# State copies of a decoder step in 56 pieces, released by the latent decode and by the last MLP

## What is computed

```python
def reference(x_prompt, x_sample, state_conv, state_swa0, state_swa1, state_swa2, state_pool, cache_mla, page_table, ...):
    for i in range(DEPTH):
        ...
        xp = xp + g1p * yp
        xs = xs + g1s * ys
        xp = xp + g2p * sq_relu_mlp(modulate(xp, norm2_g[i], sh2p, sc2p), mlp_w1[i], mlp_w2[i])
        xs = xs + g2s * sq_relu_mlp(modulate(xs, norm2_g[i], sh2s, sc2s), mlp_w1[i], mlp_w2[i])

def swa_decode(h, bufs, w_qkv, qn_g, kn_g, w_o):
    ...
        kf = jnp.concatenate([buf[:, :, 0].astype(k.dtype), k[:, :, g]], axis=1)
        vf = jnp.concatenate([buf[:, :, 1].astype(v.dtype), v[:, :, g]], axis=1)
        ...
        keep = min(w, lb + s)
        states.append(jnp.stack([kf[:, lb + s - keep:], vf[:, lb + s - keep:]], axis=2))
```

## Time and profile before

| what | value |
|---|---|
| median of 3 runs | 2119.54 us |
| lowest and highest run | 2116.04 and 2130.07 us |
| the profiled execution, its own time | 2127.36 us |
| its span, first to last instruction | 2125.8 us |
| TensorE (PE) busy | 1928.3 us, 91% |
| VectorE (DVE), ScalarE (ACT), GpSimd (POOL) busy | 1122.3, 779.5, 23.8 us |
| mean granted clock of TensorE | 0.94 of full speed |
| moved by DMA | 408.74 MB, of which 60.28 by GpSimd's queue |

### The profile page before, as it was taken

How to read it: one execution, slowest core, us unless ns; L and a number is a source line. 1 busy time by engine, 2 the same in 40 slices (tenths; PEclk the granted TensorE clock), 3 DMA queues, 4 the chain that set the end, 5 groups by cost and what they waited for, 6 DMA issues and landing times.

```text
span 2125.8 us, 32739 instructions
## 1 busy us (share of the span) xinstructions
PE 1928.3 (91%) x12829; PEld 1663.7 (78%) x12829; DVE 1122.3 (53%) x1869; ACT 779.5 (37%) x1515; POOL 23.8 (1%) x44
## 2 busy tenths in 40 slices
PE   5999999999997789999869999896899797789997
PEld 2876999989985559999749999743599696579997
DVE  4365554459744456543475544487556363365542
ACT  2312543244423234432224433343246363145432
POOL 0000000000000000000000000000000000000000
PEclk7999999999988999999989999996799898799999
DMA  9666666643441995656636656431058787434442
GB/s 358 238 238 219 220 216 218 218 158 120 165 182 50 405 335 187 230 205 218 209 116 235 212 211 209 169 103 52 1 176 291 240 268 231 149 117 144 154 149 74
DMA packets 227862, 408.74 MB, mean 192 GB/s; under 512 B 9944, under 2 KB 208639, under 8 KB 210689
## 3 DMA queue, kind: packets, MB, share of 16 engines
q1 hardware_dynamic: 223888, 341.08, 46.6%
q0 software_dynamic: 2384, 60.28, 8.3%
q10 hardware_dynamic: 1449, 5.39, 0.7%
HBM read 400.67 MB, written 60.28 MB: 217 GB/s over the span
## 4 chain that ended last, share of the span: by engine, by line
PE 72%; DVE 10%; SPq 6%; DMA 6%; issue 3%; ACT 3%; POOL 0%; ACTq 0%; DVEq 0%; POOLq 0%
PE bank L1163 40%; PE bank L1069 12%; PE bank L1138 3%; PE bank L1082 3%; DMA work<-in_pages_rope 3%; SPq L574 3%; DMA work<-in_keys_turned 2%; PE bank L1277 2%; DVE rstd L1818 2%; PE bank L1549 2%; SPq L577 2%; SPq L567 1%; DMA work<-in_ada_w 1%; PE bank L1034 1%; PE bank L1326 1%
## 5 line engine op out<-in xcount | busy, mean ns | idle before, releaser
L1673 DVE TENSOR_TENSOR ring_lo<-ring,ring_hi 128x1024 fp32r<-128x1024 f32 (+1 forms) x324 | 380.1, 1214 | 338.3 <-ACT ring_hi L715 338.3
L715 ACT ACTIVATE ring_hi<-ring 128x1024 fp32r<-128x1024 f32 (+1 forms) x324 | 323.2, 1046 | 300.9 <-PE bank L1163 283.2
L1163 PE MATMUL bank<-hidden_hi,ring_hi 128*128 128x320 f32 x1024 | 319.2, 312 | 0.0
L1163 PE MATMUL bank<-hidden_hi,ring_lo 128*128 128x320 f32 x1024 | 316.4, 309 | 0.0
L1163 PE MATMUL bank<-hidden_lo,ring_hi 128*128 128x320 f32 x1024 | 316.3, 309 | 0.0
L1163 PE MATMUL bank<-h_hi,ring_hi 128*128 128x320 f32 x896 | 279.9, 312 | 0.1
L1163 PE MATMUL bank<-h_lo,ring_hi 128*128 128x320 f32 x896 | 276.3, 308 | 0.0
L1163 PE MATMUL bank<-h_hi,ring_lo 128*128 128x320 f32 x896 | 275.9, 308 | 0.0
L1163 PEld LDWEIGHTS bank<-hidden_hi,ring_hi 128*128 128x128 f32 x1024 | 192.2, 188 | 22.6 <-issue 22.6
L1163 PEld LDWEIGHTS bank<-hidden_lo,ring_hi 128*128 128x128 f32 x1024 | 192.3, 188 | 0.0
L1163 PEld LDWEIGHTS bank<-hidden_hi,ring_lo 128*128 128x128 f32 x1024 | 192.2, 188 | 0.0
(11 more groups left out here) (276 smaller groups left out, 3121.3 us busy)
## 6 DMA issues: line engine op xcount, KB each, us to landing
ring<-in_mlp_w SPq DMA_DIRECT2D x128, 1024.0 KB, 5.5
work<-in_ada_w SPq DMA_DIRECT2D x92, 1024.0 KB, 7.1
ring<-in_swa_w_qkv SPq DMA_DIRECT2D x18, 1024.0 KB, 5.0
out_swa_old<-in_state_swa POOLq DMA_DIRECT2D x8, 2016.0 KB, 10.6
ring<-in_conv_w_in SPq DMA_DIRECT2D x12, 1024.0 KB, 5.5
work<-in_keys_turned SPq DMA_DIRECT2D x8, 1280.0 KB, 13.0
work<-in_keys_turned SPq DMA_DIRECT2D x8, 1024.0 KB, 15.0
ring<-in_values_blocked SPq DMA_DIRECT2D x4, 2048.0 KB, 11.5
```

The lines of the kernel that those rows point to most:

```text
L715: act.activation(ring_hi[:, place, part], ring[:, s, part], ACT.Copy).then_inc(sem("weights_hi"), 1)
L1163: mm = pe.matmul(bank[a % 4][:, 0:T], w[:, k, :], x(k), start=first and k == 0 and j == 0, stop=last and k == KD - 1 and j == 2)
L1673: dve.tensor_tensor(ring_lo[:, s, part], ring[:, s, part], ring_hi[:, place, part], ALU.subtract)\
```

## The change

The three copies of a sample become seven pieces: one of 480 KB, two of 1008 KB, four of 1024 KB, 56 in all. The loop over samples goes; GpSimd's program is written out. The first 28 pieces (samples 0 to 3) wait for `md_keys`, one behind every second page of the latent decode, the first of them behind page 0. The other 28 (samples 4 to 7) wait for `unit_done`, one behind each of the first 28 units of the last MLP. Nothing else is changed.

```diff
--- before.py
+++ after.py
@@ -79,6 +79,9 @@
         _u, _c, _e = _u + len(_k), _c + sum(_k), _e + sum(max(x - 1, 0) for x in _k)
 
 SWA_OLD = [min(k, min(w, k + SS) - SS) for k, (w, _) in zip(SWA_KEEP, SWA)]
+ROLL_PIECES = [(0, 0, SWA_OLD[0])] + [(1, r, SWA_OLD[1] // 2) for r in (0, SWA_OLD[1] // 2)] \
+    + [(2, r, SWA_OLD[2] // 4) for r in range(0, SWA_OLD[2], SWA_OLD[2] // 4)]
+assert all(sum(n for h, _, n in ROLL_PIECES if h == g) == SWA_OLD[g] for g in range(G))
 OLD_WORDS = OLD_BLOCKS * SWA_W
 NEAR_WORDS = 5 * SWA_W
 
@@ -615,16 +618,12 @@
         @block.gpsimd
         def _(gp):
             gp.memset(vec_in[0:64, 2, :], 0.0).then_inc(sem("vec_cleared"), 1)
-            def roll():
-
-                with gp.Fori(0, NS) as n:
-                    gp.wait_ge(sem("md_scored"), n + 1)
-                    for g in range(G):
-                        rows, lost = SWA_KEEP[g], SWA_KEEP[g] - SWA_OLD[g]
-                        gp.dma_start(O[f"swa{g}_old"][bass.ds(n, 1)].rearrange("n l k h d -> (n l) (k h d)"),
-                                     A[f"state_swa{g}"][0, bass.ds(n, 1), lost:rows].rearrange("n l k h d -> (n l) (k h d)"))\
-                          .then_inc(sem("stored"), 16)
-                stores[0] += G * NS
+            def roll(n, piece):
+
+                g, row, rows = piece
+                lost = SWA_KEEP[g] - SWA_OLD[g]
+                store(gp, O[f"swa{g}_old"][n, row:row + rows].rearrange("l k h d -> l (k h d)"),
+                      A[f"state_swa{g}"][0, n, lost + row:lost + row + rows].rearrange("l k h d -> l (k h d)"))
 
             store(gp, O["pool_s"][0, :, 0:HIST - SS], A["state_pool"][0, :, SS:HIST])
             gp.wait_ge(sem("conv_state_out"), 2)
@@ -652,7 +651,14 @@
             gp.wait_ge(sem("rope_done"), 1)
             gp.dma_start(O["latents_turned"], ml_lat).then_inc(sem("latent_rows_stored"), 16)
             gp.dma_start(O["ropes_turned"], ml_rope[0:ROPE, :]).then_inc(sem("latent_rows_stored"), 16)
-            roll()
+            pieces = [(n, piece) for n in range(NS) for piece in ROLL_PIECES]
+            half = len(pieces) // 2
+            for i in range(half):
+                gp.wait_ge(sem("md_keys"), 2 * i + 2)
+                roll(*pieces[i])
+            for i in range(half):
+                gp.wait_ge(sem("unit_done"), UNIT0["mlp1_3"] + i + 1)
+                roll(*pieces[half + i])
 
             gp.wait_ge(sem("y_copied"), 6)
             store(gp, O["y_prompt"].rearrange("a (t p) d -> p (a t) d", p=P), y_out[:, 0:2, :])
```

## The result

The changed kernel takes 2106.39 us, the median of 10 runs (2103.82 to 2111.96), and the kernel before 2127.43 (10 runs, 2116.04 to 2130.07): a ratio of 0.9913, with a 95% interval of 0.9896 to 0.993. By that ratio, which is estimated from all the runs and is not the quotient of the two medians, it is 0.9% faster. The forecast was 2090 and the range 2080 to 2112: the direction was right, and somewhat more than half of the forecast gain came. The profiled execution took 2107.65 us, 19.7 less than the one of before, and its span is 2105.9.

The account below looks back on a forecast made before the run. TensorE was taken to bound the kernel, with decode stalls from state copies: 2127.4 - 33.4 = 2094.0 us, other terms zero. The middle between 2086.1 and 2094 gave 2090 us, range 2080 to 2112.

Parts of the forecast that it names:

- What bounds the kernel: Latent decode: TensorE sets 29.78 us per sample; state copies delay page loads until TensorE stalls, an excess of 33.4 us.
- A hold of 3 us is too short for a block … So I expect no block, a set of 24 us: Decode: spread pieces would not block SyncE's page issues, leaving five to six microseconds to spare per sample; minus 33.4 us.
- My low bound: Decode: block shrinks only with the bytes, 7.1 us per sample; 6 us of lag covered, otherwise 16.7 us of stall stays.
- once enough loads are outstanding: Decode: SyncE's next issue was said to block then, for 9.33 and 3.17 us in one sample before the change.
- Two of my own signs: Decode: SyncE page issues all under 2 us if right; a sample over 31 us if wrong.
- One page of latents and ropes is 320 packets: Decode: packet count of a page, from which the loads were said to all but stand still until a copy ends.
- A page load can be held for some 3 us and not 20: Decode: one piece every 7.45 us, 16 rows, one per engine, so a page load is held only briefly.
- Rival A: Decode: pages still starve beside a single piece, sets stay late, half the stall remains, 2111 us; chance 12%.
- The last MLP: 28 pieces beside its weight loads stay hidden, zero cost: units 7.04 us, engines 90% busy, 8.7 us to spare.
- Rivals B and C: Last MLP: B, a memory limit, 2102 us, 5%; C, loads and copies take turns, 2210 us, 7%.
- Issue … Zero: GpSimd: 56 copy issues instead of 24, about 0.5 us each, where it does nothing else; no cost.
- The baseline: Profiled execution lies 7.8 us above the median of the runs; the middle of 2086.1 and 2094 was taken, 2090.

## Why the prediction was right in sign and too large

- **What bounds the kernel: right.** The stall of the old decode is the copies' doing, and 33.4 us is its size (33.5 by the run without copies).
- **"A hold of 3 us is too short for a block … So I expect no block, a set of 24 us": wrong, and this is the step that failed.** I took the block to need a stretch of many microseconds of starved loads, because the earlier trace rows show one 7.5 us behind a release. A piece of long runs with nothing queued behind it stops SyncE some two microseconds after its release, for 2.4 us on average. Four make 9.5 us in a sample; the set is 32 to 35 us. My low bound, a block that shrinks with the bytes, was 7.1 us, a set of 30.6 us and 6 us of lag; the measured lag reached 22.5, and the lead was spent one sample before the end of the decode. Of 33.4 us 26.1 came. The condition that I gave for a block, "once enough loads are outstanding", was read off the rows and never measured: in the change the stop at 1579.31 comes with the second page of its set. Two of my own signs told it: page issues of more than 2 us, and a sample of more than 31 us (37.0).
- **"One page of latents and ropes is 320 packets": a misreading, without effect.** The 2944 packets of the earlier trace rows are 8 pages with their row loads, 2.36 MB. The 192 packets and 0.16 MB of the earlier trace rows are about one whole page of latents and ropes (128 + 32 KB), in 11.4 us; that the loads all but stood still holds.
- **"A page load can be held for some 3 us and not 20": right.** Landings are 2.5 us, and the chain's longest rope page 4.88. Rival A expected late sets because the loads starve; the sets were late because SyncE did not issue, so its 2111 was nearer to the time than its mechanism was to the cause.
- **The last MLP: right.** Hidden, units of 7.04 us, landings of 7.9 us within the 6 to 9, at a DMA share of 0.82 where I had 0.9. Rivals B and C fell. In the 200 us shown, 26.66 MB of copies, read and written, and 28.53 MB of loads are (2 x 26.66 + 28.53) / 200 = 409 GB/s of memory, and no unit moved. The ceiling of 358 GB/s that the Trainium skill (DMA: Bandwidth & Descriptors, Specifications) gives, from which the prediction worked out 2121, was passed without a cost.
- **"Issue … Zero": wrong by 2.7 us.** See the last section: the price isn't at the issue, but behind the last store.
- **The baseline.** I took half of the difference between the median of 3 runs and the profiled execution off the sum. The median of 10 runs, 2127.43, equals the profiled execution. 2094.0 was the right sum, and 4 us of the error are of this step.

From 2094.0: +7.3 for the stall that stayed, +2.7 at the end, +3.5 in stretches that the change doesn't touch (ahead of the decode and in its tail, where the traces of this study differ as much: the decode begins at 1536 to 1547 us, and 84.8 to 86.9 us lie between its end and the products of the last MLP) make 2107.5, and the profiled execution took 2107.65.

## What to carry to other kernels

Where background copies share the DMA engines with loads that an engine issues just in time, look at the issuing engine's own rows first: a load that lands quickly may still have been issued late. Cut the copies into short runs before you cut or pace them; here runs of 2 to 4 KB left no stall in either of the two placements that were tried, while pacing with long runs left 7 of 33 us unwon. If long runs must stay, let the loop of loads regain its lead: one big release every second sample (2092.1 and 2094.6 us) beat four small ones in each of seven (2106.4 and 2105.6).

## What the runs showed of the hardware

**A copy costs time at the program's end.** The last store's issue on GpSimd (start, length), in four kernels. Before, with a span of 2125.8 us:

```profile
2117.50 0.54 POOL L348 DMA_DIRECT2D out_y_sample<-work  x1
```

After, with a span of 2105.9 us:

```profile
2094.94 0.54 POOL L351 DMA_DIRECT2D out_y_sample<-work  x1
```

Without copies, 2090.8 us:

```profile
2084.42 0.54 POOL L351 DMA_DIRECT2D out_y_sample<-work  x1
```

With the small copies behind the pieces, 2094.5 us:

```profile
2081.24 0.54 POOL L351 DMA_DIRECT2D out_y_sample<-work  x1
```

From that issue to the end are 8.30, 10.96, 6.38 and 13.26 us, with 24, 56, 0 and 84 copies; the store itself lands in 4.9 us each time. (13.26 - 6.38) / 84 = 0.08 us per copy, and the other two lie on the same line; so do thirteen more traces of this study, with 24 to 56 copies, within 0.3 us. All the copies had landed long before. What the chip does in this time was not tried. 28 more copies are 2.3 us by it, and the run with the small copies has a median 2.3 us above that with the pieces out of the decode, which ran on another chip.

**Long packets of one queue hold back another queue.** In the earlier trace rows the copies' queue has 96 packets of 37.5 KB on average and 91.9% of the time, the loads 192 packets and 4.6%. The Trainium skill (DMA: Bandwidth & Descriptors, Queues, rings and completion order) lets an engine change between queues only at the end of a packet, which agrees with these rows: few, long packets on one side hold back many short ones on the other. With packets of 4.7 KB (13.50 MB in 2848) a page still landed in 13.1 us beside a whole release, so short packets alone did not make the loads fast; they kept the issuing engine from being stopped.
